# Keys and values of the memory computed between the expert pairs, the first attention begun with the memory heads, and the first gather split by pair

## The reference, cut to what matters

```python
def hierarchical_moe(x2, ...):                 # per token: 2 of 32 experts
    ...                                        # 1024 -> 512 (gate, up) -> 1024 (down)
    hb = jax.nn.silu(xb @ w_gate[e]) * (xb @ w_up[e])
    return (hb @ w_down[e]) * g[:, None]

def memory_attention(qm, mem, w_mem_kv):       # once per layer, two layers
    km, vm = jnp.split(mem @ w_mem_kv, 2, axis=-1)      # mem 256x1024, w 1024x512
    ...                                                 # 4 heads of 64
    p = jax.nn.softmax(lg, axis=-1)
    o = jnp.einsum('bhsm,bmhd->bshd', p, vm)
```

## Time and profile before

| | us |
|---|---|
| median of 3 runs (lowest, highest) | 1398.41 (1397.78, 1399.11) |
| the profiled execution, its own time | 1393.92 |
| its span in the trace | 1392.2 |
| PE busy | 1211.5 (87%) |
| DVE, ACT, POOL busy | 468.4, 266.8, 320.7 |
| DMA moved | 335.76 MB |

### The profile page before, as it was taken

One profiled execution on the slowest core, in us unless ns is written; L12 is line 12 of the kernel. 1 busy time (PEld: TensorE's weight loads), 2 busy tenths in 40 slices (PEclk: granted clock), 3 DMA queues, 4 the chain that ended last, 5 costly groups with the idle time before them and its releaser, 6 DMA issues.

```text
span 1392.2 us, 18472 instructions
## 1 busy us (share of the span) xinstructions
PE 1211.5 (87%) x7489; PEld 789.1 (57%) x7497; DVE 468.4 (34%) x1160; ACT 266.8 (19%) x686; POOL 320.7 (23%) x336
## 2 busy tenths in 40 slices
PE   7999998865566655668999989999999999999997
PEld 6774555321222212122777559999448665999843
DVE  3343524110101101010205655444574213544467
ACT  4313432000000000001314541111003322111100
POOL 5000100000000000000002244888200113878800
PEclk9999999978878888779999999999999999999999
DMA  9643356999999999999937018555334038555400
GB/s 343 199 164 121 121 201 259 412 428 427 429 429 428 427 428 429 426 425 415 343 121 242 1 51 281 185 181 182 137 136 152 0 112 283 194 169 182 152 1 30
DMA packets 102505, 335.76 MB, mean 241 GB/s; under 512 B 6728, under 2 KB 58240, under 8 KB 88349
## 3 DMA queue, kind: packets, MB, share of 16 engines
q1 hardware_dynamic: 99814, 326.33, 61.0%
q0 software_dynamic: 2416, 8.30, 1.7%
q10 hardware_dynamic: 199, 0.06, 0.0%
HBM read 333.59 MB, written 2.86 MB: 242 GB/s over the span
## 4 chain that ended last, share of the span: by engine, by line
PE 69%; DMA 19%; DVE 4%; POOL 3%; issue 2%; ACT 2%; SPq 1%; POOLq 0%; DVEq 0%; ACTq 0%
PE bank L1645 18%; PE bank L860 17%; DMA ring<-in_w_expert_up 17%; PE bank L1695 8%; PE bank L1215 5%; PE bank L1233 3%; PE bank L1808 2%; PE bank L1114 2%; PE bank L1619 2%; DMA ring<-in_w_expert_down 1%; PE bank L1483 1%; PE bank L1242 1%; PE bank L1031 1%; PE bank L1540 1%; PE bank L1823 1%
## 5 line engine op out<-in xcount | busy, mean ns | idle before, releaser
L860 PE MATMUL bank<-wide_rows,ring 128*128 128x256 f32 (+3 forms) x608 | 134.9, 375 | 1.9 <-DVE arena L2370 1.7
L1645 PE MATMUL bank<-R,arena 128*128 128x128 f32 x1056 | 125.1, 275 | 0.0
L1215 PE MATMUL bank<-ring,arena 128*32 128x512 f32 x512 | 73.0, 724 | 59.7 <-DMA ring<-in_w_expert_up 59.7
L860 PEld LDWEIGHTS bank<-wide_rows,ring 128*128 128x128 f32 (+1 forms) x608 | 111.7, 191 | 23.3 <-issue 6.1
L1645 PEld LDWEIGHTS bank<-R,arena 128*128 128x128 f32 x1056 | 121.5, 192 | 0.0
L1215 PE MATMUL bank<-wide_rows,arena 128*32 128x512 f32 x128 | 70.5, 704 | 54.0 <-DMA arena<-in_w_expert_up 54.0
L3087 POOL DMA_DIRECT2D wide_rows<-in_g_final x1 | 0.6, 575 | 469.5 <-PE bank L1233 469.5
L2616 DVE TENSOR_TENSOR arena<-arena,bank 64x512 f32<-64x512 f32 x16 | 11.1, 691 | 285.2 <-ACT arena L2069 285.2
L1645 PE MATMUL bank<-wide_rows,ring 128*128 128x128 f32 x704 | 91.2, 275 | 1.0 <-ACT arena L1859 0.7
L1645 PEld LDWEIGHTS bank<-wide_rows,ring 128*128 128x128 f32 x704 | 84.8, 192 | 2.2 <-ACT wide_rows L2052 1.1
L3106 POOL TENSOR_TENSOR arena<-arena,small 128x512 f32<-128x512 f32 (+1 forms) x44 | 38.1, 866 | 193.3 <-DVE small L2794 152.7
(11 more groups left out here) (367 smaller groups left out, 1950.4 us busy)
## 6 DMA issues: line engine op xcount, KB each, us to landing
ring<-in_w_expert_down SPq DMA_DIRECT2D x29, 2048.0 KB, 14.2
ring<-in_ffn_w_in SPq DMA_DIRECT2D x44, 1024.0 KB, 8.1
ring<-in_w_expert_gate SPq DMA_DIRECT2D x16, 2048.0 KB, 23.1
ring<-in_w_expert_up SPq DMA_DIRECT2D x16, 2048.0 KB, 31.9
arena<-in_w_expert_up SPq DMA_DIRECT2D x14, 2048.0 KB, 30.8
ring<-in_ffn_w_out SPq DMA_DIRECT2D x10, 2048.0 KB, 7.7
ring<-in_w_in SPq DMA_DIRECT2D x7, 2048.0 KB, 16.0
arena<-in_w_expert_gate SPq DMA_DIRECT2D x7, 2048.0 KB, 25.7
```

Of the source, the lines that this page charges most:

```text
L860: last = pe.matmul(dst, lhsT, rhs, start=k == 0, stop=k == len(pairs) - 1)
L1215: last = pe.matmul(bank[e % 2][at:at + SLOTS, :], xg_tile(e % 2, k)[:, SLOTS * r:SLOTS * r + SLOTS], w[r][:, kk, :], start=k == 0, stop=k ...
L1645: last = pe.matmul(up_banks[layer][u % 4][i][:, at * P:(at + 1) * P], weights(k), columns(k), start=k == 0, stop=k == KT // 2 - 1)
```

## The change

Five edits, in the order of the diff.

1. The ring no longer carries the memory. The second block's list begins with `a_in` 0 to 2, `cmp_k`, `cmp_v`; four of its places are `free`. SP loads `a_in` 2, 1, 0, then the made keys and values from DRAM, then `cmp_k`, `cmp_v` and the two `a_out`.
2. SP loads the memory rows (1 MB) into `X` after the loads of pair 2. In quads 1 and 2, taken out of the loop, it loads one layer's memory weights (2 MB, rows of 2 KB) into ring slot 0 between gate/up and down of the odd pair. Slot 0 gets its expert weights for the even pair only after the products of the memory (`mem_made`), behind the loads for slots 1 to 3 and ahead of those for slots 4 and 5.
3. PE transposes the memory at the start of quad 1 and computes 32 matmuls of 256 columns per layer behind `moe_turn` of the odd pair, before its `moe_down`. ACT copies each result to three small places, POOL stores them to DRAM (`by_memory`, 12 DMAs, 1 MB in all), and SP reads them back in one DMA of 1 MB after the experts.
4. The first attention starts with `a_qm`, computed for one token block at a time, and runs steps 0 to 3 (memory heads) between the projections. The start of the feed-forward network has no memory products and orders `first_columns` anew.
5. The first gather is split: pair 0's 64 columns before its `gate_up`, pair 1's after it and before `moe_turn`.

```diff
-    order += [("mem", 0), ("mem_kv_a", 0), ("a_in", 0), ("a_in", 1), ("a_in", 2), ("cmp_k", 0)]
-    order += [("mem", 1), ("a_out", 0), ("cmp_v", 0), ("mem_kv_b", 0), ("a_out", 1)]
+    order += [("a_in", 0), ("a_in", 1), ("a_in", 2), ("cmp_k", 0), ("cmp_v", 0), ("free", 5)]
+    order += [("a_out", 0), ("free", 1), ("free", 2), ("a_out", 1), ("free", 4)]
...
-    return [("a_q", 0), ("a_kv", 0), ("a_q", 1), ("a_q", 2), ("a_kv", 1), ("cmp_h", 0), ("a_qm", 0), ("cmp_hT", 0), ("step", 0),
-            ("a_v", 0), ("cmp_kv", 0), ("step", 1), ("mem_a", 2), ("cmp_l", 0), ("mem_a", 3), ("step", 2), ("mem_b", 0), ("step", 3),
-            ("step", 4), ("mem_b", 1), ("step", 5), ("cmp_pT", 0), ("step", 6), ("summed", 6), ("step", 7), ("step", 8), ("summed", 7),
+    return [("a_qm", 0), ("a_kv", 0), ("step", 0), ("a_q", 0), ("step", 1), ("cmp_h", 0), ("step", 2), ("a_q", 1), ("cmp_hT", 0),
+            ("step", 3), ("a_v", 0), ("cmp_kv", 0), ("a_q", 2), ("cmp_l", 0), ("a_kv", 1), ("step", 4), ("step", 5), ("cmp_pT", 0),
+            ("step", 6), ("summed", 6), ("step", 7), ("step", 8), ("summed", 7),
...
+            sp.dma_start(X[:, :, :], mem_2[0].rearrange("(b p) d -> p b d", p=P)).then_inc(mem_in, 16)
+            def mem_weights(layer, i):
+                used_up(0, i * 2 + 1)
+                src = kmaj((a_w_mem_kv_2, b_w_mem_kv_2)[layer][0])
+                sp.dma_start(slot(base, src.shape[1], src.shape[2]), src).then_inc(mem_weights_in, 16)
+            def odd_pair(i, memory=None):
                 for u in range(6):
+                    if u == SPARES and memory is not None:
+                        mem_weights(memory, i)
                     used_up(u, i * 2 + (0 if u < SPARES else 1))
                     next_unit(u, i * 2 + 1, u < SPARES)
...
+            for layer in range(2):
+                odd_pair(1 + layer, memory=layer)
+                even_pair(1 + layer, (1, 2, 3))
+                sp.wait_ge(mem_made, 2 * layer + 2)
+                even_pair(1 + layer, (0, 4, 5))
+            with sp.Fori(3, LAST_QUAD) as i:
...
-            for u in (0, 1, 2, 3, 4, 5, 8, 9, 10, 7):
+            for u in (2, 1, 0):
+                load(second + u)
+            used_up(1, DUOS)
+            sp.wait_ge(mem_stored, 16 * 3 * 4)
+            sp.dma_start(arena_and_mem[:, ARENA:ARENA + half_unit], by_memory).then_inc(mem_back, 16)
+            for u in (3, 4, 6, 9):
                 load(second + u)
...
+            def gather_pair(r, done):
+                for k in range(KT):
+                    at = (k % 4) * P + r * DUO
+                    last = product(bank[2 + k // 4][:, at:at + DUO],
+                                   [(R[:, tb, k * P:(k + 1) * P], pick[:, tb, r * DUO:(r + 1) * DUO]) for tb in range(TB)])
+                    if k % 4 == 3:
+                        last.then_inc(done, 1)
...
+                if memory == 0:
+                    mem_columns()
                 moe_gate_up(1, 0, i, first)
...
                 moe_gather(1, i)
                 moe_turn(1, i)
+                if memory is not None:
+                    for side in range(2):
+                        mem_product(memory, side)
                 moe_down(1, i, first)
...
-            gather(0, moe["gathered"]).then_inc(moe["gathered"], 1)
+            gather_pair(0, first_gathered)
             moe_gate_up(0, 0, 0, first=True)
             moe_gate_up(0, 1, 0)
+            pe.wait_ge(moe["picks"], 2)
+            gather_pair(1, moe["gathered"])
             moe_turn(0, 0)
...
-            normed_to_cols("xTa", 0)
+            keep_awake(6, jobs.bank("xTa", 2))
+            for tb in range(TB):
+                turn_block("xTa", tb, 0)
...
+            first_project_a(0)
+            wait_emptied(pe, "xTa", 2)
+            wait_emptied(pe, "xTa_last")
+            first_project_a(1).then_inc(job_done, 1)
...
-                early = 2 + layer
+                early, behind = (((0, 1), (0, 1)), ((2, 0), (3, 1), (2, 1), (3, 0))) if layer == 0 else (((0, 1, 2), (0, 1, 2)), ((3, 0), (3, 1)))
...
+            for n in range(4):
+                layer, side = divmod(n, 2)
+                pool.wait_ge(mem_staged, n + 1)
+                for at, w, v in mem_stage:
+                    to = (2 * side + layer) * HALF + at
+                    pool.dma_start(by_memory[:, to:to + w], v).then_inc(mem_stored, 16)
             pool.wait_ge(moe["down"], 2 * DUOS)
```

More of the change, by code:

```diff
@@ L656, in _ @@
                 last_job["w_in", c] = job
-            for c, job in ((0, ("a_q", 1)), (1, ("a_kv", 1)), (2, ("a_v", 0))):
+            for c, job in ((0, ("a_q", 1)), (1, ("a_kv", 1)), (2, ("a_kv", 1))):
                 last_job["a_in", c] = job
@@ L671, in wait_read @@
                     sp.wait_ge(wT_used, 2 * SB_HEADS)
-                elif (what, c) == ("mem", 0):
-                    return
+                elif (what, c) == ("free", 5):
+                    sp.wait_ge(moe["down"], 2 * DUOS)
                 elif (what, c) == ("b_out", 1):
@@ L1717, in ffn @@
                     turn_block(name, 1, ahead)
-                for what, part in between(name, 1):
-                    mem_product(what, part)
+                    for u, j in behind[:2]:
+                        first_columns(u, j)
                 wait_emptied(pe, name, 2)
                 wait_emptied(pe, name + "_last")
-                for what, part in between(name, 1):
-                    wait_emptied(pe, what, part)
-                for u in range(early, 4):
-                    for j in range(2):
-                        first_columns(u, j)
+                for u, j in behind[2 - 2 * layer:]:
+                    first_columns(u, j)
                 for u in range(FFT):
@@ L2056, in empty_normed @@
                         norm_root(k_norm, 1)
-                    for what, part in between(name, tb):
-                        mem_kept(what, part)
             act.wait_ge(router_arg, 1)
@@ L2084, in moe_turned, with mem_columns, mem_out, moe_quad @@
                 turned(e).then_inc(moe["turned_copied"], 1)
-            def moe_quad(i, first=False):
+            def mem_columns():
+                for j in range(4):
+                    act.wait_ge(mem_turned, j + 1)
+                    act.activation(X[:, :, j * MEM:(j + 1) * MEM], bank[2 + j % 2][:, :].rearrange("p (a t) -> p a t", t=T),
+                                   ACT.Copy).then_inc(mem_kept, 1)
+            def mem_out(n):
+                act.wait_ge(mem_made, n + 1)
+                if n:
+                    act.wait_ge(mem_stored, 16 * 3 * n)
+                for at, w, v in mem_stage:
+                    last = act.activation(v, bank[2 + n % 2][:, at:at + w], ACT.Copy)
+                last.then_inc(mem_staged, 1)
+            def moe_quad(i, first=False, memory=None):
+                if memory == 0:
+                    mem_columns()
                 moe_silu(1, i, first)
                 moe_turned(1, i, first)
+                if memory is not None:
+                    for side in range(2):
+                        mem_out(2 * memory + side)
                 moe_silu(2, i)
@@ L2094, in _ @@
             moe_quad(0, first=True)
-            with act.Fori(1, LAST_QUAD) as i:
+            for layer in range(2):
+                moe_quad(1 + layer, memory=layer)
+            act.wait_ge(mem_stored, 16 * 3 * 4)
+            with act.Fori(3, LAST_QUAD) as i:
                 moe_quad(i)
@@ L2593, in picks @@
                 return last
[L2595 removed]
+            picks(slice(0, 2)).then_inc(moe["picks"], 1)
             weight = sm(200, 64)
@@ L2670, in _ @@
             moe_hidden(0, 0, first=True)
+            for j in range(2):
+                dve.wait_ge(moe["gathered"], j + 1)
+                take_gathered(j, (1,)).then_inc(moe["taken"], 1)
             moe_quad(0, first=True)
```

142 lines of the change are left out of this document (65 added, 77 removed).

## The result

The changed kernel takes 1405.11 us (median of 9 runs, 1397.78 to 1406.89), the kernel before, run beside it, 1397.78 (9 runs, 1390.08 to 1399.97). The ratio is 1.0058, 95% interval 1.0041 to 1.0075: it is slower, by some 8 us. Forecast were 1396.9 and a range up to 1405, so the sign is the other one and the time is 0.11 above the range.

The account below looks back on a forecast made before the run. DMA engines bound the expert stage, PE what follows. +20.2 us in the first and -21.7 behind it gave -1.5: 1392.4 profiled, 1396.9 as median, range 1388.5 to 1405.

Parts of the forecast that it names:

- A load that is late next: Behind the experts, `cmp_h` needs `cmp_v`, landing at about 695.4: PE waits 3, plus 1.7 for the clock, 4.9 in all.
- the new waits on copies: First attention: PE waits where a product's copy is needed at once, before `cmp_l`, step 4 and step 5; 0.7 each, 2.2.
- SP waits for the products: Expert stage: DMA engines run dry while SP waits for `mem_made` after pairs 3 and 5; +3.2 us, bounds 0 and 7.2.
- Bytes and stores: Expert stage: memory rows and two layers of memory weights add +13.5 us, POOL's stores of 1.05 MB +2.0.
- Split gather: Start of the expert stage: `down` of pair 0 comes 1.8 later, deepening the DMA hole at 260; +1.5 us, bounds 0 and 1.8.
- Start of the feed-forward network: From the transposes to `up`, 10.5 us instead of 16.8 without memory products; -6.3, bounds -5 and -7.
- A: Faster: SP's wait for the products is covered, the clock holds, the hole at 260 is absorbed; 1388.8 us, chance 0.28.
- B: Slower: slot 0's load and everything of SP behind it wait for the 32 products; 1401 to 1409, taken as 1405, chance 0.12.
- C: Expert stage: POOL's small stores cost the skill page's price for small DMAs, +9.8; 1406.7 us, chance 0.05.
- D: First attention: steps 0 to 3 between projections make PE wait 1 us more at five places; +5, 1402 us, chance 0.10.
- the hole behind the products: Sign: a hole of 1 to 3 us in the DMA rate about 31 us after pair 3's and pair 5's landings.
- the wait of `cmp_h`: Sign: PE waiting for `cmp_v` about 37 us after the last expert load's landing; without it the prediction is wrong.

Follow-up runs that it names:

- the early products: Changed kernel with memory weights loaded between the odd pair's second and third unit and the 32 products computed before its `gate_up`: 1393.91 us, ratio 0.9999.
- second profiles: Changed kernel and kernel before, both unaltered, each profiled a second time: 1405.71 and 1398.60 us.

## Why the prediction was wrong

Its mechanisms were found where it put them, but two terms that both stand against the change were too small, and the net of -1.5 was a small difference of sums of 20. The step that failed first is **"A load that is late next"**: "PE waits 3, and I add 1.7 for the clock after that idle time: 4.9 in all". The runs show 11.6 in its place (step 6 at 91.0 behind the landing in the changed kernel against 79.4 with `cmp_h` later):

- The wait is 6.4 to 6.5, not 3. PE reached `cmp_h` earlier than forecast, 33.0 behind the landing (720.95 - 687.99) instead of 34.8, since the opening on `a_qm` ran at full clock (7.31, beside 7.07 for the same work in the earlier trace rows). And `cmp_v` came 39.3 behind it instead of 37.7: I had carried over the 26.4 of the earlier trace rows for "also 11.2 MB"; what makes the 1.6 isn't shown.
- The clock is 4.4, not 1.7. I had one disturbed row in mind, as the 5.41 in the earlier trace rows; in the changed kernel `cmp_h` loses 2.8 and `a_kv` 1, 37 us later, loses 1.6, and both are back at full speed when the wait is filled.
- Without that wait the forecast would have been 81.8 behind the landing (86.7 less 4.9), and the runs give 79.4. The rest of that part was right and a little too low in gain; the new waits on copies (0.73, 0.75, 0.42) are the size forecast.

The second is **"SP waits for the products"**, "+3.2"; 6.1 by the early products. The path of PE was right (30.7 forecast, 31.0 measured: 303.5, which is 0.35 ahead of PE's first matmul, to 334.53). But the engines ran dry at 332.1, 28.6 after the landing and not 30.0, and after the issue they moved half the bytes of full rate for 3.4 us. The sum had everything behind `mem_made` start again at once; in fact slots 4 and 5 have to wait 3.6 us more, for the odd pair's `down` that the products push back, and for this wait there was no term. How the excess of 2.9 divides between the earlier dry point, the slow restart and the wait for `down` isn't separated: the early products take all three away. The upper bound, 7.2, held the value.

The other terms:

- *Bytes and stores* 15.5 (13.5 + 2.0): measured 16.4, the kernel with late `cmp_h`, early products and split (450.87 from gather to landing) against the split alone (434.47). Right within 1; and 23.0 of the table is 16.4 + 6.1 + 0.5.
- *Split gather* +1.5: `down` 1.9 later, as forecast, but only 0.4 to 0.5 of it is left at the last landing in executions where the low clock misses the gather, as less time passes there from issue to landing: 396.9 from issue to landing with the split alone, 397.3 and 398.5 in the two profiles without it. By the ratios it is 2.4 (1.0058 - 1.0041), 3.1 (1.0022) and 5.8 us. These three and the 0.5 don't meet. The record has one candidate: where the low clock falls on the gather, the split cost 3.9 at the landing. How often that happens in the runs that weren't profiled isn't known, nor whether the late start is more frequent with the split, so the difference stays open. The forecast had no term for the clock here.
- *Start of the feed-forward network* -6.3: -6.4.

Of the rivals, A (more is covered) is out: 6.1 lost where it had 0, and the clock not held. B named the right place, the slot handed back late, and its restart price (+4, 1401) is of the size of the measured excess of 2.9 there, which holds the wait for `down` as well; its low clock during the products wasn't seen (7.17 and 7.07). C is out by the doubled stores. D is out: the moved steps pay a little more than forecast once `cmp_h` stands later. What none of the cases had is the sum that came about: two waits, each underpriced in the same direction. Of the signs named ahead, the hole behind the products and the wait of `cmp_h` came, and pair 3's first matmul came 4.2 later (301.86 against 297.69 in the second profiles), as forecast. The sizes told of the miss: step 6 at 91.0 instead of 86.7 behind the landing, and the expert stage, which was to grow by 15 to 26, grew by 23.0 in the second profiles and by 29.7 in the first.

## What to carry to other kernels

When work is pulled forward, work out anew the place of every consumer of a load behind it: here the gain was real (21 us from landing to step 6 with `cmp_h` later, 100.4 to 79.4), and one list entry two places too early gave half of it back. Price a new wait of PE with the low clock after it, in all the rows that follow and not in the next one alone. Price a new wait of the load queue with the slow restart of a single transfer, and look at what the loads behind it wait for, as that may have moved too (here `down`). And give moved work an existing idle place (PE's wait for the odd pair's loads) and not the gap just ahead of what the queue waits for: with `cmp_h` two places later, the products in the wait ahead of them and the first gather whole, the kernel is 1.0% faster than before instead of 0.6% slower.

## What the runs showed of the hardware

- Runs of one kernel spread over 4 to 11 us, and the longer ones have the lower mean granted clock. Over 159 runs of ten kernels a line through each kernel's own runs gives 0.92 us (standard error 0.05) per 0.001 of mean clock. The low stretch ahead of the experts falls on the identity matmuls (5.4 to 6.2 instead of 3.70), on the gather (5.47 instead of 3.84) or, with the half gather, on gather and `gate_up` (6.35 and 9.40), of the same kernel in different executions.
- A wait of PE of 6.35 us is followed by 2.8 us lost in the next 64 records, and 1.6 in a product 37 us later; with zeros in the wait both are gone (7.09, 7.13).
- After an empty queue, one 2 MB load with three small stores beside it moved 0.74 MB in the 3.4 us after its issue, half of what 428 GB/s is.
- Twelve stores of 64 and 128 KB beside full queues cost their bytes, 2.8 us per 1.05 MB, not a price each.
